# Recurrent mixer: sums of squares and spreads by quarters of the array in two banks, level products over all 64 columns

## The reference, cut to what matters

```python
kk = heads(k * k_k)
kk = kk / jnp.maximum(jnp.sqrt(jnp.sum(kk * kk, axis=-1, keepdims=True)), 1e-12)
...
def step(state, inp):                       # 256 steps
    sa = jnp.einsum('bhvk,bhk->bhv', state, -kk_t)
    state = (state * w_t[:, :, None, :] + sa[..., None] * (kk_t * a_t)[:, :, None, :]
             + v_t[..., None] * k_t[:, :, None, :])
    return state, jnp.einsum('bhvk,bhk->bhv', state, r_t)
...
mean = jnp.mean(y, axis=-1, keepdims=True)
var = jnp.mean(jnp.square(y - mean), axis=-1, keepdims=True)
yn = ((y - mean) * lax.rsqrt(var + RWKV_LN_EPS)).reshape(B, S, RWKV_WIDTH)
```

## Time and profile before

| | us |
|---|---|
| median of 3 runs | 2650.13 (2650.01 to 2650.53) |
| profiled execution | 2648.62 |
| its span (first to last instruction) | 2646.8 |
| PE busy | 2620.4 (99% of the span) |
| DVE busy | 1929.2 (73%) |
| ACT busy | 1383.2 (52%) |
| rounds of the mixer | from about 295 to 429 of the span |

### The profile page before, as it was taken

The page is one execution under the profiler, slowest core; times in us unless marked ns, Lnnn a source line. Parts: engine busy times, 40 slices in busy tenths (PEclk is TensorE's granted clock), DMA queues, the critical chain, the costliest instruction groups (busy, mean ns, idle before and its releaser), DMA issues.

```text
span 2646.8 us, 46069 instructions
## 1 busy us (share of the span) xinstructions
PE 2620.4 (99%) x16930; PEld 2258.2 (85%) x16930; DVE 1929.2 (73%) x2947; ACT 1383.2 (52%) x2153; POOL 148.5 (6%) x162
## 2 busy tenths in 40 slices
PE   9999999999999999999999999999999999999998
PEld 8888888889888888888888888888888888888886
DVE  6778676877877877878887666588877656765676
ACT  6555555676544534535565454345455535553554
POOL 5600002201000000000000000000000000000000
PEclk9999999999999999999999999999999999999999
DMA  7555103556788887888778855687665655555554
GB/s 264 178 188 175 58 4 137 176 186 225 266 299 280 287 294 280 291 285 281 281 273 305 292 173 183 201 278 279 245 207 191 193 191 189 190 193 191 189 192 151
DMA packets 159504, 578.42 MB, mean 219 GB/s; under 512 B 18224, under 2 KB 18768, under 8 KB 158288
## 3 DMA queue, kind: packets, MB, share of 16 engines
q1 hardware_dynamic: 156224, 563.59, 61.8%
q10 hardware_dynamic: 2080, 9.46, 1.0%
q0 software_dynamic: 1008, 2.71, 0.4%
HBM read 572.81 MB, written 2.11 MB: 217 GB/s over the span
## 4 chain that ended last, share of the span: by engine, by line
PE 95%; DVE 2%; issue 1%; ACT 1%; POOL 1%; DMA 0%; SPq 0%; ACTq 0%; DVEq 0%; POOLq 0%
PE ps L2742 34%; PE ps L2746 18%; PE ps L2824 12%; PE ps L2825 12%; PE ps L2826 12%; PE ps L1151 1%; PE ps L1802 1%; PE ps L1164 0%; POOL ssm L1900 0%; DVE wlo L2282 0%; DMA raw<-in_stream 0%; PE ps L1100 0%; PE ps L2807 0%; PE ps L2809 0%; PE ps L2808 0%
## 5 line engine op out<-in xcount | busy, mean ns | idle before, releaser
L2282 DVE TENSOR_TENSOR wlo<-raw,whi 128x1024 fp32r<-128x1024 f32 x872 | 1059.0, 1230 | 515.6 <-ACT whi L1933 512.4
L1933 ACT ACTIVATE whi<-raw 128x1024 fp32r<-128x1024 f32 x871 | 904.5, 1057 | 780.2 <-PE ps L2746 371.7
L2742 PE MATMUL ps<-xn,whi 128*128 128x512 f32 x3760 | 941.1, 392 | 2.2 <-ACT whi L1933 0.9
L2742 PEld LDWEIGHTS ps<-xn,whi 128*128 128x128 f32 x3760 | 674.7, 188 | 122.6 <-issue 2.2
L2746 PEld LDWEIGHTS ps<-xn,wlo 128*128 128x128 f32 x3760 | 510.8, 191 | 37.1
L2746 PE MATMUL ps<-xn,wlo 128*128 128x256 f32 x3760 | 520.5, 282 | 0.0
L2824 PE MATMUL ps<-whi,act_in 128*128 128x512 f32 x1120 | 436.1, 389 | 0.0
L2825 PE MATMUL ps<-wlo,act_in 128*128 128x512 f32 x1120 | 435.7, 389 | 0.0
L2826 PE MATMUL ps<-whi,act_in 128*128 128x512 f32 x1120 | 435.7, 389 | 0.0
L2824 PEld LDWEIGHTS ps<-whi,act_in 128*128 128x128 f32 x1120 | 210.2, 188 | 44.7 <-DVE wlo L2282 1.0
L2826 PEld LDWEIGHTS ps<-whi,act_in 128*128 128x128 f32 x1120 | 210.2, 188 | 43.7
(11 more groups left out here) (344 smaller groups left out, 2230.3 us busy)
## 6 DMA issues: line engine op xcount, KB each, us to landing
raw<-in_stream SPq DMA_DIRECT2D x872, 512.0 KB, 4.2
adaw<-in_ada SPq DMA_DIRECT2D x96, 512.0 KB, 5.6
adaq<-in_ada SPq DMA_DIRECT2D x96, 512.0 KB, 5.2
h<-in_xT SPq DMA_DIRECT2D x8, 256.0 KB, 9.1
memx<-in_memT ACTq DMA_DIRECT2D x1, 2048.0 KB, 9.0
gate_row<-gates POOLq DMA_DIRECT2D x2, 1024.0 KB, 7.2
lwa<-in_lora ACTq DMA_DIRECT2D x2, 512.0 KB, 4.4
lwa<-in_lora ACTq DMA_DIRECT2D x1, 1024.0 KB, 7.7
```

The lines of the kernel that those rows point to most:

```text
L1933: act.activation(whi[:, r, :], raw[:, r, :], ACT.Copy).then_inc(hi_done, 1)
L2282: dve.tensor_tensor(wlo[:, r, :], raw[:, r, :], whi[:, r, :].bitcast(F32), ALU.subtract)\
L2742: return pe.matmul(ps[:, lin.bank(g, t), :], whi[:, (p0 + s) % RING, c * 512 + t * P:c * 512 + (t + 1) * P], x[:, 2 * s + c, :], start=s + ...
```

## The change

The sums of squares become eight matmuls of a quarter of the array each (`head_sums`): 64 rows of one head, 64 tokens as stationary operand, one moving column. The sums of the two heads, which are two row halves of the array, go to two different banks. The spreads become eight quarter matmuls with 64 moving columns (`spread`); the halves of the tokens, again two row halves, go to two different banks. DVE therefore reads two banks, with two instructions where it had one, in `norm_k_d`, `key_d`, `variance` and `normed`. Since the banks now hold both lanes' data for the key and for the output's spread, several waits are for both lanes: `norm_k_t` for `zw`, `gate_t` for `km`, `spread_k_t` for `gg`, `norm_k_d` for `kn`, `key_d` for `rb`, `normed` for `vb`. The first step of the state (L1223) waits for `n2` where it waited for `n1`, which DVE does just before `n2`.

The products of `first` and of the levels move all 64 columns in order, so their results lie unpacked in PSUM, and ACT and DVE pick the chosen columns out of PSUM with a stepped read. Stationary operands, the number of these matmuls and what ACT and DVE write stay.

```diff
-    def spread_bank(i, g):
-        return ps[:, 4 * g + (3 if i < 3 else 2), 0:T]
-
-    def sums_of(i, g):
-        return bank(i, g, "kn")[:, 0:4]
+    pair = lambda first, step: [first, first + step]
+    KEY_SUMS = lambda i: pair(2, 4) if i else pair(0, 2)
+    KEY_SPREAD = lambda i: pair(2, 4) if i else pair(4, 2)
+    DEV_SUMS = lambda i, g: pair(4 * g, 1 if i < 3 else 2)
+    DEV_SPREAD = lambda i: pair(3 if i < 3 else 2, 4)
+    DEV_AT = 448
+
+    by_half = lambda x, t: x.rearrange("p (b t c) -> p t b c", b=2, t=2)[:, t, :, :]
+    spread_of = lambda bank, g: ps[:, bank, g * P:(g + 1) * P].rearrange("p (b c) -> p b c", b=2)
...
                 CT.wait(act, g, i, f"p{lv}")
-                CA.done(act.activation(half(pp[g][:, :, :], lv, 0), packed(ps[:, 4 * g, 0:P], lv), ACT.Copy), g, f"c{lv}")
+                CA.done(act.activation(half(pp[g][:, :, :], lv, 0), half(packed(ps[:, 4 * g, 0:T]), lv, 0), ACT.Copy), g, f"c{lv}")
...
     def norm_k_d(dve, i):
+        for z in lanes:
+            PT.wait(dve, z, i, "kn")
+            if i == 0:
+                PA.wait(dve, z, i, "gg")
         for g in lanes:
-            PT.wait(dve, g, i, "kn")
-            if i == 0:
-                PA.wait(dve, g, i, "gg")
-            pd(dve, i, g, "km", dve.tensor_scalar(rk[2 * (i % 2) + g][:, 0:4], sums_of(i, g), 1e-24, None, ALU.max))
+            for hd in range(2):
+                ins = dve.tensor_scalar(rk[2 * (i % 2) + g][:, hd:4:2], ps[:, KEY_SUMS(i)[hd], g * P:g * P + 2], 1e-24, None, ALU.max)
+            pd(dve, i, g, "km", ins)
...
     def key_d(dve, i):
+        for z in lanes:
+            PT.wait(dve, z, i, "rb")
         for g in lanes:
             n = 2 * i + g
-            PT.wait(dve, g, i, "rb")
-            pd(dve, i, g, "kk", dve.scalar_tensor_tensor(kk[i][g][:, :], tiles(n)[1], col("k_k", n), bank(i, g, "rb")[:, 0:T],
-                                                    ALU.mult, ALU.mult))
+            for t in range(2):
+                ins = dve.scalar_tensor_tensor(by_half(kk[i][g][:, :], t), by_half(tiles(n)[1], t), col("k_k", n),
+                                               spread_of(KEY_SPREAD(i)[t], g), ALU.mult, ALU.mult)
+            pd(dve, i, g, "kk", ins)
...
-                                                       ps[:, 4 * g:4 * g + 2, w * P:w * P + CH].rearrange("p h (b c) -> p h b c", b=2)))
+                                                       ps[:, 4 * g:4 * g + 2, w * P:(w + 1) * P].rearrange("p h (b c k) -> p h b c k", b=2, k=2)[:, :, :, :, w]))
...
-                        packed(ps[:, 4 * g + 1, 0:P] if w else ps[:, 4 * g, T:T + P], lv)))
+                        half(packed(ps[:, 4 * g + 1, 0:T] if w else ps[:, 4 * g, T:2 * T]), lv, w)))
...
-                yd_(i, g, "ve", dve.tensor_scalar(rv[g][:, 0:4], ps[:, 4 * g, T:T + 4], 1.0 / CH, EPS_HEAD, ALU.mult, ALU.add))
+                for hd in range(2):
+                    ins = dve.tensor_scalar(rv[g][:, hd:4:2], ps[:, DEV_SUMS(i, g)[hd], DEV_AT:DEV_AT + 2],
+                                            1.0 / CH, EPS_HEAD, ALU.mult, ALU.add)
+                yd_(i, g, "ve", ins)
...
-                YT.wait(dve, g, i, "vb")
-                yd_(i, g, "yn", dve.scalar_tensor_tensor(y, y, col("lnx_w", n), spread_bank(i, g), ALU.mult, ALU.mult), True)
+                for z in lanes:
+                    YT.wait(dve, z, i, "vb")
+                for t in range(2):
+                    ins = dve.scalar_tensor_tensor(by_half(y, t), by_half(y, t), col("lnx_w", n), spread_of(DEV_SPREAD(i)[t], g),
+                                                   ALU.mult, ALU.mult)
+                yd_(i, g, "yn", ins, True)
...
+    quarters = [(b, hd, th) for b in range(2) for hd in range(2) for th in range(2)]
+
+    def head_sums(pe, banks, at_col, x):
+        for b, hd, th in quarters:
+            ins = pe.matmul(ps[rows(th), banks[hd], at_col + b:at_col + b + 1], x[rows(hd), b * P + th * CH:b * P + (th + 1) * CH],
+                            blk[rows(hd), 0, hd * CH:hd * CH + 1], start=True, stop=True)
+        return ins
+
     def norm_k_t(pe, i):
         for g in lanes:
             PA.wait(pe, g, i, "kq")
             if i:
-                CA.wait(pe, g, i - 1, "zw")
-            for b in range(2):
-                ins = pe.matmul(sums_of(i, g)[:, 2 * b:2 * b + 2], kq[i][g][:, b * P:(b + 1) * P], blk[:, 0, 0:P:CH],
-                         start=True, stop=True)
-            PT.done(ins, g, "kn")
+                for z in lanes:
+                    CA.wait(pe, z, i - 1, "zw")
+            PT.done(head_sums(pe, KEY_SUMS(i), g * P, kq[i][g]), g, "kn")
...
-                PD.wait(pe, g, i, "km")
+                for z in lanes:
+                    PD.wait(pe, z, i, "km")
             pe.matmul(bank(i, g, "g")[:, T:2 * T], lwa(n, 2), lora_in(1), start=True, stop=False)
...
-    def spread(pe, out, x):
-        for b in range(2):
-            for hd in range(2):
-                ins = pe.matmul(out[rows(hd), b * P:(b + 1) * P], x[:, 2 * b + hd:2 * b + hd + 1].to_broadcast([P, CH]), ident[:, :],
-                         start=True, stop=True)
+    def spread(pe, banks, g, x):
+        for b, hd, th in quarters:
+            o = g * P + b * CH
+            ins = pe.matmul(ps[rows(hd), banks[th], o:o + CH], x[rows(th), 2 * b + hd:2 * b + hd + 1].to_broadcast([CH, CH]),
+                            ident[rows(th), th * CH:(th + 1) * CH], start=True, stop=True)
         return ins
...
-                PA.wait(pe, g, i, "gg")
-            PT.done(spread(pe, bank(i, g, "rb")[:, 0:T], rk[2 * (i % 2) + g][:, 4:8]), g, "rb")
+                for z in lanes:
+                    PA.wait(pe, z, i, "gg")
+            PT.done(spread(pe, KEY_SPREAD(i), g, rk[2 * (i % 2) + g][:, 4:8]), g, "rb")
...
-                    o = P * turned + CH // 2 * b
+                    o = P * turned + CH * b
                     n_, t_ = av[rows(hd), c ^ 1, :], bk[q][rows(hd), 0, CH * c:CH * c + CH]
-                    ins = mm(ps[rows(cc ^ turned), 4 * g + hd, o:o + CH // 2], t_ if turned else n_,
-                             n_[:, 1:CH:2] if turned else t_[:, 0:CH:2], start=True, stop=True)
+                    ins = mm(ps[rows(cc ^ turned), 4 * g + hd, o:o + CH], t_ if turned else n_,
+                             n_ if turned else t_, start=True, stop=True)
...
-                        ins = mm(ps[rows(1 - cc), 4 * g, u * HC:(u + 1) * HC], lm[g][rows(cc), hd, b, 0:CH],
-                                 half_of(xx[g][rows(cc), 0, u, :], lv, 0), start=True, stop=True)
+                        ins = mm(ps[rows(1 - cc), 4 * g, u * CH:(u + 1) * CH], lm[g][rows(cc), hd, b, 0:CH],
+                                 xx[g][rows(cc), 0, u, :], start=True, stop=True)
...
-                            mm(ps[k, 4 * g, T + u * HC:T + (u + 1) * HC], xx[g][f, 1, u, :], half_of(pp[g][f, u, :], lv, 0),
+                            mm(ps[k, 4 * g, T + u * CH:T + (u + 1) * CH], xx[g][f, 1, u, :], pp[g][f, u, :],
                                start=True, stop=True)
-                        ins = mm(ps[f, 4 * g + 1, u * HC:(u + 1) * HC], pp[g][f, u, :], half_of(xx[g][f, 1, u, :], lv, 1),
+                        ins = mm(ps[f, 4 * g + 1, u * CH:(u + 1) * CH], pp[g][f, u, :], xx[g][f, 1, u, :],
                                  start=True, stop=True)
...
-                    CD.wait(pe, g, i, "n1" if c == 1 else "s2")
+                    CD.wait(pe, g, i, "n2" if c == 1 else "s2")
...
-                for b in range(2):
-                    ins = mm(ps[:, 4 * g, T + 2 * b:T + 2 * b + 2], yq[g][:, b * P:(b + 1) * P], blk[:, 0, 0:P:CH],
-                             start=True, stop=True)
-                YT.done(ins, g, "va")
+                YT.done(head_sums(pe, DEV_SUMS(i, g), DEV_AT, yq[g]), g, "va")
...
-                YT.done(spread(pe, spread_bank(i, g), rv[g][:, 4:8]), g, "vb")
+                YT.done(spread(pe, DEV_SPREAD(i), g, rv[g][:, 4:8]), g, "vb")
```

More of the change, by code:

```diff
@@ L400, in half_of, with packed @@
         return x.rearrange("p (n k b) -> p n k b", k=2, b=1 << lv)[:, :, w, :]
-    def packed(x, lv):
-        return x.rearrange("p (a n b) -> p a n b", a=4, b=1 << lv)
+    def packed(x):
+        return x.rearrange("p (a c) -> p a c", a=4)
     def scalar(act, split_first):
@@ L1094, in tensor @@
         mm = pe.matmul
-        HC = CH // 2
         four = [(hd, b) for hd in range(2) for b in range(2)]
```

## The result

The changed kernel takes 2654.19 us (median of 22 runs, 2650.49 to 2656.99), the kernel before 2650.14 (22 runs): ratio 1.0015, interval 1.0009 to 1.002. It is about 4 us slower, where 2.7 us less were forecast, and outside the range that was given.

The account below looks back on a forecast made before the run. PE was taken to hold 95% of the chain, with DVE's fixed order deciding which savings count. Rounds 1 and 2 1.60, round 0 0.65, round 3 −0.20, preparation 0.65: 2.70 us gain, median 2647.4, own range 2645.5 to 2649.0.

Parts of the forecast that it names:

- the pace of quarter passes: Sums and spreads on PE: 32 passes take 0.48 us on four quarters, each step saving about 0.5.
- I leave the clock out of the sum: Whole kernel: PE's clock was taken to stay at the upper of two levels throughout, so it got no term.
- Between the rounds: Before `lora_t`, rounds 0 to 1 and 1 to 2: gain 0.65 us each, limited by DVE's `yn`; PE idle 0.85.
- Round 0's key sums: In round 0, with no `yn` to wait for, the shorter key sums gain their full 0.5 us.
- The key's spread: Before `doubled` of level 3: 0.5 us shorter on PE, of which 0.30 counts in rounds 0, 1 and 2.
- Hand-overs: PE to ACT in the levels: 0.03 us later for wider results, five per round, costing 0.15 in each of four rounds.
- Stepped reads: ACT and DVE picking columns out of PSUM: between 0 and 8.1 us for some 54 reads, taken as nothing.
- rivals c and d: c: single-element reads in `first` cost 1.8 us, 2649.2, chance 0.16; d: every stepped read pays, 8.1 us, 2655.5, chance 0.08.
- `n2`: First state step waiting for `n2`: costs 0.20 us in round 3, nothing in rounds 0 to 2.
- Round 0's preparation: Key sums and spread in the input projection: 0 to 1.0 us shorter in all, 0.65 taken.

Follow-up runs that it names:

- b_pad208: The kernel before with 208 more PE instructions at its start (four warm-up matmuls replaced by 56 quarter matmuls): 2652.47 us, ratio 1.001 to before.
- a_pad32: The changed kernel with 32 more PE instructions at its start, nothing else different: 2649.70 us, ratio 0.9999 to the kernel before.
- a_pad96: The changed kernel with 96 more PE instructions at its start, nothing else different: 2650.08 us, ratio 1.0001 to the kernel before.
- levels_only: The kernel before with only the 64-column products and their stepped PSUM reads, sums and spreads as before: 2650.35 us, ratio 1.0005 to before.
- p32_n1: a_pad32 with the first step of the state waiting for `n1` again: 2648.85 us, ratio 0.9999 to the kernel before.
- a_pad256: Control: the changed kernel with 256 more PE instructions at its start, a whole block: 2655.64 us, ratio 1.0022 to the kernel before.
- sums_only: The kernel before with only the quarter sums and spreads and their waits, products of 32 columns as before: 2655.84 us, ratio 1.0022 to before.
- b_lora: The kernel before with `lora_t` moved behind the first `doubled` of its round: 2650.78 us, ratio 1.0007 to before.

## Why the prediction was wrong

The step that failed is the one from the pace of quarter passes to the sum. "32 passes on four quarters cost about 4 × 0.12 = 0.48" was right (0.45 for the sums); I then took it that PE can keep that pace up for as long as instructions stand in the program, and gave the waiting for them no term. Each of the first three rounds now has 80 passes more, 160 instructions, in less time, and other borders of blocks. The holes grew by 4.63 − 0.27 = 4.36 us, which alone turns the forecast gain into a loss. A second term was put at nothing: "I leave the clock out of the sum", because it had stood at the upper level before. It fell, and that cost 1.17 us in the rounds of the profiled execution, and a part of the 1.38 lost behind them. With both taken off, the 4.00 us that the rounds lost are a gain of 1.5, where 2.05 were forecast for them. The kernel before showed the same holes, 0.175 us in the middle of L1205 at 388.85, too small to be asked about; and the padding shows that it had borders that happened to cost little (b_pad208). None of my rivals was this mechanism.

Step by step:
- Between the rounds, 0.65 each: `lora_t`'s matmuls start at 337.06, 1.20 later than before, where the sums had started 1.64 later (331.26 against 329.62): 0.44. The new wait is there (PE idle 1.04, I had said 0.85). The rest went into the split `normed`: I took 0.49 for two halves from an operation of 128 columns, and it took 0.60; why is not shown.
- Round 0's key sums, 0.5: `lora_t`'s first load 301.84 before, 301.42 after, with the round starting 0.10 later: 0.52. Right.
- The key's spread, 0.30: in round 1 `product` of level 3 was 1.34 late and that of level 4 1.26, with a hole of 0.35 between: 0.43. Near enough. DVE still stood idle for 0.22 there, but behind that hole; in a_pad32 and a_pad96, which have no hole at this place, it does not wait before level 3's writes at all, as forecast (a_pad32, DVE; the writes follow the operation ahead without a gap).

```profile
344.47 0.48 DVE L807 SCALAR_TENSOR_TENSOR bp<-proj,par,tb 128x256 f32<-128x256 f32 x1
344.87 0.90 DVE L867 COPY_PREDICATED xx<-mk,ps 128x128 f32<-128x128 int32 x4
```

- Hand-overs −0.60: −0.5 to −0.8 in levels_only. Right. Stepped reads nothing: right, so rivals c and d fall. The Trainium skill's "Advanced Engine Details and Errata", section Memory Cachelines, wants pairs of elements adjacent; the reads of single elements by DVE in `first` took 1.27 before and after.
- `n2`: 0.20 in round 3 was right (the row below, which follows 0.19 of waiting); that it costs nothing in the other rounds was wrong at least in round 1, which takes 0.25 more in a_pad32 than in p32_n1.

```profile
426.52 0.33 PE L1247 MATMUL ps<-nn,mt 64*64 64x64 f32 x4 [0.19 <-DVE nn L884]
```

- Round 0's preparation, 0.65: nothing. The first load of `bonus_t` stands at 274.84, before at 274.83, as the chain goes through ACT and DVE just ahead of it; what PE saves earlier ends in that wait.

With the borders moved and the clock up, the mechanism is seen at half to four fifths of the size that I gave it. The rounds of a_pad32 are 136.64 us long with 1.43 of holes, those of before 137.13 with 0.27, so 1.65 us less without the holes; a_pad96 gives 1.08 in the same way. The forecast for the rounds was 2.05. Taking off a hole's idle time is an estimate, since another engine may have been what the path waited for.

## What to carry to other kernels

An engine's own instruction stream is a resource: before a few slow instructions are replaced by many fast ones, look in the trace for idle time inside a run of one line, released by "issue", and count whether its places are a fixed number of instructions apart. Where they are, padding by a fraction of a block, and by a whole block as the control, separates this loss from the edit's own worth. And where one step ends earlier, the next wait behind it on the same queue (here `lora_t` for `yn`) takes the gain unless what stands behind it is let past.

## What was not expected of the hardware

- A 16 KB packet of PE's instructions was entered 2.2 us or more after its transfer began, and up to 1.35 us of waiting in one place followed from that (b_pad208).
- Behind holes and waits of PE the granted clock fell to 1.2 GHz for 3.4 us, or twice that, in several profiles (after, a_pad256, sums_only); one such stretch cost 1.17 us in after. Not every wait did it: a_pad96 waited 0.69 in a hole, and the kernel before 2.13 for DVE, and the clock stayed up. In b_lora it fell at 370.6 with no wait over 0.06 us in the 3 us ahead. What share of the 4 us it makes over all runs was not measured by itself.
- DVE's and ACT's reads of PSUM with gaps, down to single float32 elements, took no longer than packed ones.
